# One inference step of a hybrid decoder: mLSTM and delta rule with tokens on partitions, head norms inside both

## The chip, the cores and the metric

The kernel runs on one core of a Trainium2 chip. The metric is the device time of one execution in microseconds. A core has TensorE for matrix products (PE in the profile, its weight loads PEld), VectorE (DVE), ScalarE (ACT), GpSimd (POOL) and a queue for transfers, SyncE (SP). Each engine works through its own instruction list; semaphores hold them together.

## The reference, cut to what matters

Two layers over a prompt of 1024 tokens and 8 sample sequences of 8 tokens, with the same weights. Layer 0 mixes with four mLSTM heads and four gated delta-rule heads; all in float32. The part around the change:

```python
# mLSTM, per chunk: b = cumsum(log f), m_t = running max
s = einsum('bthd,bshd->btsh', qc, kc) * exp(d - m_t)
num = einsum('btsh,bshv->bthv', s, vc) + a_inter * einsum('bthd,bhdv->bthv', qc, c)
den = sum(s, axis=2) + a_inter * einsum('bthd,bhd->bth', qc, n)
h = num / maximum(abs(den), exp(-m_t))
hm = rmsnorm(h, mi_norm) * sigmoid(mo)            # per head of 128
# delta rule, per chunk
v_new = u_c - w_c @ s
o = qd_c @ s + at_c @ v_new
s = exp(gl_c) * s + kd_c.T @ v_new
og = rmsnorm(o, gd_norm) * silu(gz)               # per head of 128
y = concatenate([hm, og]) @ w_out
```

## The kernel before

Activations lie transposed, features on the 128 partitions and the 1088 tokens (padded to TP = 1092) along the free dimension. Z has 20 such tiles: 0-3 the mLSTM queries and keys, 4-7 its values and then its outputs, 8-11 delta queries, 12-15 keys, 16-19 values and then outputs. Tokens go in 8 chunks of 128 (NC = 8) and one chunk of 64 for the sample group, which the code calls chunk NC. Layer 0 is a row of stages, and each stage ends with a barrier of all engines: products (input projection), mlstm, delta, headnorm, wout0 (output projection).

**mlstm** (L463) runs the prompt's chunks first and the sample chunk last. In each, TensorE makes the scores ST with the keys as weights, spreads three rows over the partitions (`bcast`, L527), turns the values (L551), and reads out with values as weights, so the outputs NUM come with features on partitions (L562, L564) and the denominator DEN, spread over all 128 partitions by a second set of products with ones (L569, L571). VectorE takes the maximum of the denominator and its bound, a reciprocal of 128x512 (L687) and the product (L689). For the sample chunk each product with a state is done for every sequence with 8 columns (L567, L574). The sample states are loaded by 20 transfers at the front (L498, L501) and stored by 20 at the end (L513, L516). Every buffer is single.

**delta** (L712) has a first part (preparation of all chunks, inverse of the 32x32 blocks on VectorE, sample group) and then a loop over the chunks. Its order on TensorE in chunk i: `new_values(i)` (L932, L937), `first(i + 1)` (L901), the state product SU (L954), `second(i + 1)` (L907, L910, L914), the outputs OUT (L961, L963) with `third(i + 1)` (L920) in their middle, `fourth(i + 1)` (L927). ScalarE turns WT and VN to SBUF (L1029, L1031) and scales the keys for the next chunk (`scaled`, L1021), which `fourth` wants. POOL makes the mask parts (`parts`, L1077), the spread inverses (L1087) and the keys at the chunk's end (L1061), which `first` and SU want. VectorE copies OUT to Z (L1197).

**headnorm** (L1603) makes for all 8 heads: squares on ScalarE (L1638), their sums over the partitions by products with a column that selects a row (L1651), root and reciprocal, the rows spread by products (L1659), two products per tile on VectorE (L1673, L1676), and the split in a high and a low half for the output projection (ScalarE L1643, POOL L1630). The gates come from DRAM in one transfer (L1622). The high halves go to Z 8-15, the low ones stay in Z 4-7 and 16-19. It also loads and splits the first weight of wout0.

## Time and profile before

| | |
|---|---|
| median of 3 runs | 4121.89 us (4121.21 to 4123.23) |
| the profiled execution | 4122.16 us, span 4120.4 us |
| PE / PEld busy | 88% / 81% of the span |
| DVE / ACT / POOL busy | 35% / 14% / 29% |
| mean granted PE clock | 0.895 of full |

The span is cut in stages by barriers, so a stage costs what the last of its engines costs, and a mean over the span tells little of it. The windows and the timeline show it stage by stage. A matmul of float32 shows as two records.

### The profile page before, as it was taken

Reading aid. Unit: us, or ns where it says so; the run is one execution under the profiler, and the core shown is the slowest. Engines: PE = TensorE matmul, PEld = TensorE weight load, DVE = VectorE, ACT = ScalarE, POOL = GpSimd, SP = SyncE. Lnnn points to the kernel's source line nnn. Section 1 sums busy time; section 2 is a strip of 40 time slices with the busy share of each in tenths; the row PEclk is TensorE's granted clock in tenths of the full one; section 3 lists DMA queues with packets and bytes.
Section 4 is the critical chain, followed back from the end, with each engine's and each line's share of the span. In section 5 each row is a group of like instructions: output and inputs, shape, how many; then the busy total and the mean of one; then the engine's idle time right before and its main releaser. Section 6 shows DMA issues by size and latency. Waiting matters only on the chain. (4 is left out here: it accounts for less than half of the span.)

```text
span 4120.4 us, 48469 instructions
## 1 busy us (share of the span) xinstructions
PE 3606.7 (88%) x20881; PEld 3348.4 (81%) x20881; DVE 1434.4 (35%) x2055; ACT 590.2 (14%) x982; POOL 1196.0 (29%) x545
## 2 busy tenths in 40 slices
PE   6999656889999999989885978799777899999998
PEld 6899555868999999988684768688555899999998
DVE  4931353533423241431001044555412342414143
ACT  4310111221100000011100023233111110000012
POOL 3433000325344344424030021111000444434442
PEclk8999875788999999999986889699755999999999
DMA  4112102212111111123113032100111211111111
GB/s 122 42 37 64 43 2 33 50 53 80 42 47 42 46 42 46 47 69 129 39 42 98 0 75 46 40 6 7 38 60 48 74 42 47 42 47 46 43 46 59
DMA packets 303612, 204.01 MB, mean 50 GB/s; under 512 B 73065, under 2 KB 283323, under 8 KB 302856
## 3 DMA queue, kind: packets, MB, share of 16 engines
q1 hardware_dynamic: 294056, 196.44, 16.6%
q10 hardware_dynamic: 9344, 4.47, 0.4%
q8 instruction: 165, 2.70, 0.3%
q14 instruction: 47, 0.39, 0.0%
HBM read 158.69 MB, written 33.40 MB: 47 GB/s over the span
## 5 line engine op out<-in xcount | busy, mean ns | idle before, releaser
L264 PE MATMUL ps<-u_r,wslots_r 128*128 128x364 f32 x4608 | 772.3, 330 | 0.0
L264 PEld LDWEIGHTS ps<-u_r,wslots_r 128*128 128x128 f32 x4608 | 770.8, 189 | 0.0
L264 PE MATMUL ps<-hn_r,wslots_r 128*128 128x364 f32 x2880 | 589.5, 331 | 11.7 <-PEq L76 11.7
L235 POOL TENSOR_TENSOR wslots_r<-rawm,sb_ones 128x1024 fp32r<-128x1024 f32 x133 | 321.2, 2415 | 912.8 <-PE ps L264 871.2
L264 PE MATMUL ps<-low_r,wslots_r 128*128 128x364 f32 x2688 | 543.6, 330 | 26.5 <-PEq L76 24.7
L264 PEld LDWEIGHTS ps<-hn_r,wslots_r 128*128 128x128 f32 x2880 | 497.1, 189 | 12.2 <-POOLq L229 12.2
L264 PEld LDWEIGHTS ps<-low_r,wslots_r 128*128 128x128 f32 x2688 | 462.0, 189 | 26.9 <-POOLq L229 24.8
L237 POOL TENSOR_TENSOR wslots_r<-rawm,wslots_r 128x1024 fp32r<-128x1024 f32 x133 | 379.1, 2851 | 10.4
L1685 DVE TENSOR_TENSOR xT<-xT,ps 128x1092 f32<-128x1092 f32 x80 | 103.4, 1292 | 667.6 <-PE ps L264 667.6
L1334 PE MATMUL ps<-hn_r,wslots_r 128*128 128x364 f32 x1392 | 278.3, 333 | 17.8 <-POOLq L1304 9.2
L1334 PEld LDWEIGHTS ps<-hn_r,wslots_r 128*128 128x128 f32 x1392 | 239.9, 191 | 24.3 <-DVE Z L1561 11.9
L2848 PE MATMUL ps<-xT 128*128 128x128 f32 (+7 forms) x1184 | 168.7, 287 | 1.9 <-DVE xT L3049 0.9
L2848 PEld LDWEIGHTS ps<-xT 128*128 128x128 f32 (+7 forms) x1184 | 152.1, 198 | 18.0 <-issue 8.7
L1334 PE MATMUL ps<-xT_r,wslots_r 128*128 128x364 f32 x696 | 155.1, 331 | 0.0
L1309 POOL TENSOR_TENSOR wslots_r<-raw,sb_ones 128x1024 fp32r<-128x1024 f32 x28 | 69.7, 2490 | 226.9 <-PE ps L1334 205.5
L1726 ACT ACTIVATE u_r<-u 128x1092 fp32r<-128x1092 f32 x32 | 35.8, 1118 | 628.3 <-DVE u L1723 628.3
L1726 ACT ACTIVATE low_r<-hn 128x1092 fp32r<-128x1092 f32 x32 | 35.8, 1118 | 627.8 <-DVE hn L1723 627.8
L1334 PEld LDWEIGHTS ps<-xT_r,wslots_r 128*128 128x128 f32 x696 | 122.6, 191 | 0.0
L2932 ACT ACTIVATE xT<-ps 128x512 f32<-128x512 f32 (+5 forms) x148 | 85.1, 598 | 172.3 <-DVE ps L3028 116.0
L264 PEld LDWEIGHTS ps<-Z_r,wslots_r 128*128 128x128 f32 x576 | 97.9, 192 | 9.6 <-POOLq L229 9.6
L264 PE MATMUL ps<-Z_r,wslots_r 128*128 128x364 f32 x576 | 98.2, 333 | 8.6 <-PEq L76 8.6
L1720 DVE TENSOR_TENSOR hn<-ps,row 128x1092 f32<-128x1092 f32 x32 | 41.5, 1296 | 184.0 <-PE ps L264 170.6
(576 smaller groups left out, 5108.2 us busy)
## 6 DMA issues: line engine op xcount, KB each, us to landing
rawm<-in_w_down SPq DMA_DIRECT2D x64, 512.0 KB
rawm<-in_w_up SPq DMA_DIRECT2D x63, 512.0 KB
raw<-in_w_in_even SPq DMA_DIRECT2D x28, 512.0 KB
xT<-x_saved SPq DMA_DIRECT2D x2, 4368.0 KB
xT<-in_cache_fox_kv SPq DMA_DIRECT2D x16, 512.0 KB
more_r<-more_r SPq DMA_DIRECT2D x28, 256.0 KB
panel_raw<-in_w_in_odd SPq DMA_DIRECT2D x6, 1024.0 KB
x_saved<-Z SPq DMA_DIRECT2D x1, 4368.0 KB
```

The costliest lines, as they stand in the source:

```text
L235: nc.gpsimd.tensor_tensor(r32(half[0][:, g % 2]), raw[:, g % 2], one, ALU.mult).then_inc(s["high"], 1)
L237: nc.gpsimd.tensor_tensor(r32(half[1][:, g % 2]), raw[:, g % 2], r32(half[0][:, g % 2]), ALU.subtract) \
L264: mm = pe.matmul(view[n % 2][:, c, :], r32(half[a][:, n % 2, k, :]), r32(t["x"][b][:, k, CH * c:CH * (c + 1)]), start=(k == 0 and (a, b) = ...
L1309: G_.tensor_tensor(r32(half[0][:, g % 2]), raw[:, g % 2], one, ALU.mult).then_inc(s["high"], 1)
L1334: mm = pe.matmul(acc[:, c, :], r32(half[a][:, g % 2, k, :]), r32((hn, low)[b][:, k, CH * c:CH * (c + 1)]), start=(k == 0 and (a, b) == HAL ...
L1685: return e.tensor_tensor(v3(xT[:, n, :]), v3(xT[:, n, :]), acc, ALU.add)
L1720: return e.tensor_tensor(v3(u[1][:, n, :]), acc, v3(row), ALU.mult)
L1726: return e.activation(r32(u[0][:, n, :]), u[1][:, n, :], ACT.Copy)
L2848: mm = pe.matmul(out(u, kind)[:, h, :], prob[0:r, n % 3, P * h:P * (h + 1)], v, start=(n == branch_first[(u, kind)] and h == 0), stop=(n = ...
L2932: nc.scalar.activation(prob[0:r, n % 3, :], S(n)[0:r], ACT.Exp).then_inc(act_.sem, act_.mark(("exp", n)))
```

## The change

Both mixers now give their outputs with the tokens on the partitions: in the read-out the decayed scores (and queries) are the weights, and values (and states) flow through. In mLSTM a 129th column of ones in the values gives the denominator in the same product. Norm, denominator and root are then factors of one column per head (128x4 for a chunk), by which a chunk is scaled; four transposes bring it back to features on partitions, where it meets its gate, comes from DRAM by chunk (18 slices in all), and is split in its high and low halves. The stage headnorm and its call are gone; the high halves lie in Z 0-3 and 8-11.

mLSTM is written anew: the sample chunk is first, buffers are double, the chunk i + 1 is prepared before chunk i is read out, sample states are updated two per chunk in the first four chunks and stored behind them. A state of 64 rows lies at partitions 0-63 or 64-127 and is multiplied there, without zero padding. For the sample chunk, queries are masked per sequence by POOL (`qm`), and states flow with 129 columns. The factor 0.125 of the keys goes into the input projection.

In delta, each chunk's squares, root and high half are on ScalarE, scaling and gating on VectorE, the transposes in `second`, the low half on POOL; the first weight of wout0 is loaded and split in its loop, and `keys_at_end(0)` stands behind the sample products on POOL.

```diff
-def mlstm(pr, I, O, C, Z, GC, RT, arena, ps):
...
+def mlstm(pr, I, O, C, Z, GC, RT, G, gam, blocks, bufs, ps):
...
+    order = [NC] + list(range(NC))
+    num = room([P, NC + 1, 4, P])
...
+            load_gate(0)
+            load_gate(1)
+            sp.wait_ge(dve_.sem, dve_.at(("Cb", NB - 1)))
+            for x in range(2):
+                sl = slice(64 * x, 64 * x + 64)
+                for b in range(NB):
+                    sp.dma_start(O["s_mlstm_c"][0, b].rearrange("(y x) d v -> x d y v", x=2)[x], Cb[sl, b, :, 0:P]).then_inc(s["st"], 16)
+                for y in range(2):
+                    sp.dma_start(O["s_mlstm_n"][0, :, 2 * y + x, :].rearrange("b (d o) -> d b o", o=1), Cb[sl, :, y, P:P + 1],
                                  allow_slow_non_contiguous=True).then_inc(s["st"], 16)
+            for k in range(2, 6):
+                load_gate(k)
...
+            for k in range(6, NC + 1):
+                load_gate(k)
+            sp.wait_ge(s["st"], 16 * 24)
...
+            def prepare(i):
+                k, r, cc = order.index(i), token_rows(i), cols(i)
+                if k:
+                    need(dve_, ("pt", order[k - 1]))
+                for h in hs4:
+                    m = pe.matmul(RB[:, h, 0:r], C["sel"][:, h, :], RT[:, cc], start=True, stop=True)
+                done(m, ("RB", i))
+                if k:
+                    need(act_, ("kt", order[k - 1]))
+                for h in hs4:
+                    pe.matmul(AB[hp(h), h // 2, 0:r], C["sel"][:, 4 + h, 0:64], RT[:, cc], start=True, stop=True)
+                for y in (0, 1):
+                    m = pe.transpose(TR[0:r, P * y:P * y + P], Z[:, 2 + y, cc], C["ident"][:])
+                done(m, ("TR", i))
+                if k:
+                    need(act_, ("vt", order[k - 1]))
+                for h in hs4:
+                    m = pe.transpose(VT[0:r, h, :], Z[:, 4 + h, cc], C["ident"][:])
+                done(m, ("VT", i))
+                need(dve_, ("D", i))
+                for h in hs4:
+                    m = pe.matmul(ST[0:r, h % 2, h // 2, 0:r], Z[hp(h), 2 + h // 2, cc], Z[hp(h), h // 2, cc], start=True, stop=True)
+                done(m, ("ST", i))
+
+            def read_out(i):
+                k, r = order.index(i), token_rows(i)
+                need(dve_, ("pt", i))
+                need(act_, ("vt", i))
+                need(dve_, "pad")
+                if k:
+                    need(dve_, ("num", order[k - 1]))
+                    need(act_, ("ssq", order[k - 1]))
+                else:
+                    need(dve_, "cols")
+                    need(dve_, "ends")
+                    pe.wait_ge(s["state"], 16 * 20)
+                    need(pool_, "qm")
+                p_, v_ = of(i, pt, pts), of(i, vt, vts)
+                if 0 < i < NC:
+                    need(dve_, ("C", i - 1))
                     need(dve_, ("qa", i))
+                for h in hs4:
+                    dst = N[h % 2][0:r, h // 2, :]
+                    m = pe.matmul(dst, p_[:, h, 0:r], v_[:, h, :], start=True, stop=not i)
+                    if 0 < i < NC:
+                        m = pe.matmul(dst, qa[hp(h), i % 2, h // 2, :], Cs[hp(h), i % 2, h // 2, :], start=False, stop=True)
+                    for b in range(NB if i == NC else 0):
+                        m = pe.matmul(dst, qm[hp(h), h // 2, b, :], Cb[hp(h), b, h // 2, :], start=False, stop=(b == NB - 1))
+                done(m, ("N", i))
...
+            prepare(NC)
+            need(dve_, "cols")
+            need(dve_, "ends")
+            prepare(0)
+            read_out(NC)
+            for i in range(NC):
+                if i + 1 < NC:
+                    prepare(i + 1)
+                if i < 4:
+                    update_sample(2 * i)
+                read_out(i)
+                update(i)
+                if i < 4:
+                    update_sample(2 * i + 1)
+                if i == 4:
+                    turn_back(0)
+                if i >= 4:
+                    turn_back(i - 3)
+            for k in range(5, NC + 1):
+                turn_back(k)
...
+            def squares(i):
+                k, r = order.index(i), token_rows(i)
+                need(dve_, ("num", i))
+                need(dve_, "clear")
+                for h in hs4:
+                    if h or k:
+                        need(act_, ("junk", k, h - 1) if h else ("ssq", order[k - 1]))
+                    ins = A.activation(junk[0:r], num[0:r, k, h, :], ACT.Square, accum_out=ssq[0:r, k, h:h + 1])
+                    step(("junk", k, h) if h < 3 else ("ssq", i), ins)
+
+            def root(n):
+                need(dve_, ("mean", n))
+                step(("root", n), A.activation(part[:, 5 * n:5 * n + 5 - n], part[:, 5 * n:5 * n + 5 - n], ACT.Sqrt))
...
+            prepare(NC)
+            prepare(0)
+            squares(NC)
+            for i in range(NC):
+                if i + 1 < NC:
+                    prepare(i + 1)
+                squares(i)
+                if i == 3:
+                    root(0)
+                if i == 4:
+                    high(0)
+                if i >= 4:
+                    high(i - 3)
+            root(1)
+            for k in range(5, NC + 1):
+                high(k)
...
+            def weigh(k):
+                r = token_rows(order[k])
+                pool.wait_ge(s[f"gate{k % 2}"], 16 * (k // 2 + 1))
+                step(("gate", k), E.tensor_tensor(gate[:, k % 2, :, 0:r], gate[:, k % 2, :, 0:r], spread(gam[:, 0:4], r), ALU.mult))
+            weigh(0)
+            weigh(1)
+            for k in range(NC + 1):
+                w = wide(order[k])
+                need(act_, ("high", k))
+                step(("low", k), E.tensor_tensor(r32(Z[:, 4:8, w]), Z[:, 4:8, w], r32(Z[:, 0:4, w]), ALU.subtract))
+                if k + 2 <= NC:
+                    weigh(k + 2)
...
+            def out(i):
+                k, r = order.index(i), token_rows(i)
+                need(pe_, ("N", i))
+                step(("den", i), V.tensor_copy(den[0:r, k].rearrange("p (y x o) -> p x y o", x=2, o=1), nums[0:r, :, :, P:P + 1]))
+                step(("num", i), V.tensor_copy(by_half(num[0:r, k]), nums[0:r, :, :, 0:P]))
+                need(dve_, ("den", i))
+                step(("minus", i), V.tensor_scalar(part[0:r, k], den[0:r, k], -1.0, None, ALU.mult))
+                need(dve_, ("minus", i))
+                step(("abs", i), V.tensor_tensor(den[0:r, k], den[0:r, k], part[0:r, k], ALU.max))
+                need(dve_, ("abs", i))
+                step(("bound", i), V.tensor_tensor(den[0:r, k], den[0:r, k], cols_of[0:r, i, 32:36], ALU.max))
+
+            def factors(n):
+                w = slice(5 * n, 5 * n + 5 - n)
+                need(act_, ("ssq", 3 + 4 * n))
+                need(dve_, ("bound", 3 + 4 * n))
+                step(("rden", n), V.reciprocal(den[:, w], den[:, w]))
+                need(dve_, ("rden", n))
+                step(("s1", n), V.tensor_tensor(part[:, w], ssq[:, w], den[:, w], ALU.mult))
+                need(dve_, ("s1", n))
+                step(("s2", n), V.tensor_tensor(part[:, w], part[:, w], den[:, w], ALU.mult))
+                need(dve_, ("s2", n))
+                step(("mean", n), V.tensor_scalar(part[:, w], part[:, w], 1.0 / P, EPS, ALU.mult, ALU.add))
+                need(act_, ("root", n))
+                step(("rroot", n), V.reciprocal(part[:, w], part[:, w]))
+                need(dve_, ("rroot", n))
+                step(("fac", n), V.tensor_tensor(fac[:, w], part[:, w], den[:, w], ALU.mult))
+
+            def scaled(k):
+                r = token_rows(order[k])
+                if k >= 2:
+                    need(pe_, ("HT", k - 2))
+                need(dve_, ("fac", 0 if k < 5 else 1))
+                step(("hs", k), V.tensor_tensor(hs[0:r, k % 2], num[0:r, k], spread(fac[0:r, k], P), ALU.mult))
+
+            def gated(k):
+                i = order[k]
+                r = token_rows(i)
+                need(pe_, ("HT", k))
+                need(pool_, ("gate", k))
+                step(("z", k), V.tensor_tensor(Z[:, 4:8, cols(i)], HT[:, :, 0:r], gate[:, k % 2, :, 0:r], ALU.mult))
...
+            for i in range(NC):
+                if i + 1 < NC:
+                    decay(i + 1)
+                if i < 4:
+                    state_sample(2 * i)
+                if i + 1 < NC:
+                    weights(i + 1)
+                out(i)
+                state(i)
+                if i < 4:
+                    state_sample(2 * i + 1)
+                if i == 3:
+                    factors(0)
+                    scaled(0)
+                    scaled(1)
+                if i == 4:
+                    gated(0)
+                    scaled(2)
+                if i >= 4:
+                    gated(i - 3)
+                    if i < 6:
+                        scaled(i - 1)
+            factors(1)
+            scaled(5)
+            scaled(6)
+            for k in range(5, NC + 1):
+                gated(k)
+                if k + 2 <= NC:
+                    scaled(k + 2)
...
+            sp.wait_ge(s["out"], 16)
+            first_load(sp, s, W, following)
+            for k in range(NC + 1):
+                if k >= 2:
+                    sp.wait_ge(dve_.sem, dve_.at(("z", k - 2)))
+                if k == NC:
+                    sp.wait_ge(dve_.sem, dve_.at(("S", NC - 1)))
+                    sp.dma_start(O["p_gdn_s"][0, 0].rearrange("h k v -> k h v"), S[:, NC % 2]).then_inc(s["last"], 16)
+                i = order[k]
+                sp.dma_start(gate[:, k % 2, :, 0:token_rows(i)], G[4:8, :, cols(i)].rearrange("h p t -> p h t")).then_inc(s[f"gate{k % 2}"], 16)
+            sp.wait_ge(s["last"], 16)
...
+                if i >= 2:
+                    turn_back(i - 2)
...
+            def turn_back(k):
+                r = token_rows(order[k])
+                need(dve_, ("hs", k))
+                if k:
+                    need(dve_, ("z", k - 1))
+                if k + 1 < NC:
+                    need(dve_, ("S", k + 1))
+                for h in hs:
+                    m = pe.transpose(HT[:, h, 0:r], turned[0:r, k % 2, h, :], C["ident"][0:r, 0:r])
+                done(m, ("HT", k))
...
                 if i:
                     need(dve_, ("S", i - 1))
+                if i >= 2:
+                    need(dve_, ("z", i - 2))
                 for h in hs:
                     m = pe.matmul(SU[:, h], kd[:, i % 2, h], vn[:, h], start=True, stop=True)
                 done(m, ("SU", i))
                 if more:
                     second(i + 1)
                 if i:
-                    need(dve_, ("O", i - 1))
+                    need(dve_, ("hs", i - 1))
+                to = OUT[(i + 1) % 2]
                 for h in hs:
-                    m = pe.matmul(OUT[:, h], vn[:, h], at[:, i, h], start=True, stop=not i)
+                    m = pe.matmul(to[:, h], at[:, i, h], vn[:, h], start=True, stop=not i)
                     if i:
-                        m = pe.matmul(OUT[:, h], S[:, i % 2, h], Z[:, 8 + h, cols(i)], start=False, stop=True)
+                        m = pe.matmul(to[:, h], Z[:, 8 + h, cols(i)], S[:, i % 2, h], start=False, stop=True)
                     if h == 1 and more:
                         third(i + 1)
...
+            for k in range(NC - 2, NC + 1):
+                turn_back(k)
...
+            def root(k):
+                i = order[k]
+                r = token_rows(i)
+                need(pe_, ("O", i))
+                need(dve_, "clear")
+                for h in hs:
+                    need(act_, ("square", k, h - 1) if h else ("square", k - 1, 3) if k else "VT")
+                    step(("square", k, h), A.activation(junk[0:r], OUT[k % 2][0:r, h, :], ACT.Square, accum_out=ssq[0:r, k, h:h + 1]))
+                need(act_, ("square", k, 3))
+                step(("root", k), A.activation(ssq[:, k], ssq[:, k], ACT.Sqrt, scale=1.0 / P, bias=eps[:, 0:1]))
+
+            def high(k):
+                w = wide(order[k])
+                need(dve_, ("z", k))
+                step(("high", k), A.activation(r32(Z[:, 8:12, w]), Z[:, 16:20, w], ACT.Copy))
...
+                root(i)
+                if i >= 2:
+                    high(i - 2)
                 if i + 1 < NC:
                     scaled(i + 1)
...
-            need(act_, ("kk", NC - 1))
-            need(dve_, ("last", NC - 1))
-            keys_at_end(0)
...
+            need(act_, ("kk", NC - 1))
+            need(dve_, ("last", NC - 1))
+            need(pe_, ("SUb", NB - 1))
+            keys_at_end(0)
...
+            def low(k):
+                w = wide(order[k])
+                need(act_, ("high", k))
+                step(("low", k), G_.tensor_tensor(r32(Z[:, 16:20, w]), Z[:, 16:20, w], r32(Z[:, 8:12, w]), ALU.subtract))
...
+                if i == 2:
+                    pool.wait_ge(s["out"], 16)
+                    first_split(nc, pool, s, W)
+                if i >= 3:
+                    low(i - 3)
...
+            def scaled(k):
+                i = order[k]
+                r = token_rows(i)
+                need(act_, ("root", k))
+                step(("rroot", k), V_.reciprocal(fac[:, k], ssq[:, k]))
+                need(dve_, ("rroot", k))
+                if k == 0:
+                    dve.wait_ge(s["out"], 16)
+                if k >= 2:
+                    need(pe_, ("HT", k - 2))
+                step(("hs", k), V_.tensor_tensor(turned[0:r, k % 2], OUT[k % 2][0:r], spread(fac[0:r, k], P), ALU.mult))
+
+            def gated(k):
+                i = order[k]
+                need(pe_, ("HT", k))
+                dve.wait_ge(s[f"gate{k % 2}"], 16 * (k // 2 + 1))
+                r = token_rows(i)
+                step(("z", k), V_.scalar_tensor_tensor(out=Z[:, 16:20, cols(i)], in0=HT[:, :, 0:r], scalar=gam[:, 4:5], in1=gate[:, k % 2, :, 0:r],
+                                                       op0=ALU.mult, op1=ALU.mult))
...
-                need(pe_, ("O", i))
-                step(("O", i), V_.tensor_copy(Z[:, 16:20, cols(i)], OUT))
...
+                if 1 <= i < NC - 1:
+                    gated(i - 1)
+                scaled(i)
...
+                    if mlstm_of.get(g) in (2, 3):
+                        step(("free", what), V.scalar_tensor_tensor(out=v3(dst), in0=acc, scalar=0.125, in1=v3(row[:]), op0=ALU.mult, op1=ALU.mult))
+                    else:
+                        step(("free", what), V.tensor_tensor(v3(dst), acc, v3(row[:]), ALU.mult))
...
-def head_norms(pr, I, Z, which, G, gates, arena, W, following, ps):
...
-            with nc.sbuf_tensor("normroom", [P, 2300], F32) as normroom:
-                head_norms(pr, I, Z, which, G, hn[:], Arena(wslots[:, 1].rearrange("p k m -> p (k m)"), spare[:], RT[:], normroom[:]), W, last, ps)
...
```

## Rows read from the trace of the kernel before

**Rows 1.** Windows: start:end, length, busy us of PE, PEld, DVE, ACT, POOL, clock, DMA share, GB/s

```profile
452.30:606.80 154.50, 86.53 (x608) 81.92 (x608) 84.19 (x157) 27.93 (x65) 0.00 (x0) 0.79 0.04 8
606.80:671.10 64.30, 49.95 (x246) 44.78 (x246) 22.41 (x73) 2.68 (x8) 0.00 (x0) 0.50 0.00 1
671.10:696.60 25.50, 0.00 (x0) 0.00 (x0) 0.00 (x0) 0.00 (x0) 0.00 (x0) 0.50 0.53 41
...
885.60:956.10 70.50, 46.79 (x96) 20.41 (x96) 31.00 (x18) 20.09 (x18) 30.80 (x10) 0.65 0.20 74
...
834.50:879.40 44.90, 42.98 (x353) 41.04 (x353) 20.67 (x40) 9.44 (x25) 14.47 (x13) 1.00 0.00 1
```

**Rows 2.** Timeline, mlstm: start, duration, engine, line, idle before and its releaser

```profile
452.34 5.24 SPq L498 DMA_DIRECT2D xT<-in_state_mlstm_c  x8
...
471.09 0.60 DVE L638 COPY xT<-Z 64x256 f32<-64x256 f32 x2
...
486.42 3.35 DVE L687 RECIPROCAL wslots<-wslots 128x512 f32<-128x512 f32 x1
...
490.41 0.60 DVE L638 COPY xT<-Z 64x256 f32<-64x256 f32 x2
```

**Rows 3.** Timeline of one chunk in the loop of delta

```profile
834.56 0.49 PE L937 MATMUL ps<-xT,hn 128*128 128x128 f32 x2 [0.46 <-ACT hn L1029]
...
836.43 0.60 ACT L1031 ACTIVATE hn<-ps 128x512 f32<-128x512 f32 x1 [1.92 <-PE ps L937]
836.57 2.16 POOL L1087 TENSOR_TENSOR hn<-xT,sb_block 128x512 f32<-128x512 f32 x2 [3.80 <-PE ps L937]
...
840.05 1.16 PE L914 MATMUL ps<-hn,Z 128*128 128x128 f32 x8
...
841.35 2.62 POOL L1077 TENSOR_TENSOR Z<-xT,sb_level 128x512 f32<-128x512 f32 x2 [1.51 <-PE ps L914]
...
843.93 1.16 PE L927 MATMUL ps<-hn,Z 128*128 128x128 f32 x8
...
845.77 0.49 PE L937 MATMUL ps<-xT,hn 128*128 128x128 f32 x2 [0.46 <-ACT hn L1029]
...
847.44 1.06 PE L901 MATMUL ps<-hn,Z 128*128 128x128 f32 x8
```

**Rows 4.** Timeline at the end of delta and the start of wout0

```profile
884.89 0.69 DVE L1197 COPY Z<-ps 128x512 f32<-128x512 f32 x1 [0.66 <-PE ps L963]
887.51 2.12 ACT L1638 ACTIVATE normroom<-Z 128x1092 f32<-128x1092 f32 x2 [5.65 <-PEq L76]
...
956.15 44.03 PE L264 MATMUL ps<-Z_r,wslots_r 128*128 128x364 f32 x250 [8.57 <-PEq L76]
```

**Rows 5.** Groups of instructions, shapes apart: count, total us, mean ns, idle before

```profile
L421 ACT ACTIVATION_READ_ACCUMULATOR Z<-Z 128x1 f32 x8 | 1.5, 193 | 0.0
L607 ACT ACT_TABLE_LOAD x1 | 1.3, 1283 | 0.0
...
L607 ACT ACTIVATE xT<-xT,GC 128x128 f32<-128x128 f32 x32 | 10.2, 390 | 2.4 <-DVE xT L644 2.4
...
L680 DVE SCALAR_TENSOR_TENSOR xT<-xT,ps 64x129 f32<-64x129 f32 x28 | 9.8, 349 | 27.9 <-PE ps L581 27.2
...
L685 DVE TENSOR_TENSOR wslots<-wslots 128x512 f32<-128x512 f32 x8 | 5.5, 692 | 0.3
...
L1119 DVE COPY xT<-hn 128x4 f32<-128x4 f32 x8 | 1.3, 162 | 0.0
...
L1050 POOL TENSOR_TENSOR Z<-Z,hn 128x512 f32<-128x512 f32 x8 | 10.2, 1276 | 23.7 <-PE ps L829 23.7
```

**Rows 6.** Transfers by line: count, KB each, us from issue to landing

```profile
out_s_gdn_s<-wslots SPq DMA_DIRECT2D x1, 2048.0 KB, 10.0
...
xT<-delta_inverse SPq DMA_DIRECT2D x16, 64.0 KB, 2.2
```

**Rows 7.** Timeline, delta: 128-row products followed by 64-row ones

```profile
705.31 0.39 PE L828 MATMUL ps<-Z 128*128 128x128 f32 x2
...
705.54 0.39 PE L829 MATMUL ps<-Z 128*128 128x128 f32 x2
...
705.85 0.67 PE L836 MATMUL ps<-hn,Z 64*64 64x64 f32 x8
```

567 lines of the change are left out of this document (251 added, 316 removed).

## The prediction

> **What bounds the kernel now.** I read four views, in this order. First the windows of layer 0's mixers. In each, the reader is to see how little of the stretch TensorE is busy, and at which clock [rows 1]. The mLSTM chunks take 154.5 us with PE busy 86.5; the sample group 64.3 us at clock 0.50; then 25.5 us pass with no engine busy, while only the stores of the sample state leave; the stage of head norms takes 70.5 us. Elsewhere PE is the bound (the delta loop: 43.0 of 44.9 us busy at clock 1.00). Second, the timeline of one mLSTM chunk [rows 2]: L638 starts at 471.09 and again at 490.41, so a chunk takes 19.3 us, and 3.35 us of it are one reciprocal of 128x512. It is a chain with no overlap: PE stands still while VectorE ends a chunk. Third, the timeline of one chunk of the delta loop [rows 3]: L937 starts at 834.56 and at 845.77, a period of 11.21 us, PE nearly without gaps. Fourth, the end of that stage [rows 4]: its last copy ends at 885.58, the next stage's first instruction starts 1.93 us later (what a stage boundary costs), and the output projection's first matmul starts at 956.15.
>
> So what counts is what ends last in each stage: in mLSTM the dependency chain, in the delta loop PE, in head norms everything, since nothing of another stage runs beside it. Stages are barriers, so each one's saving adds to the others.
>
> **mLSTM, front.** The state loads come first, as now: eight issues take 5.24 us [rows 2], 0.655 each. 21 of them (20 and the new block mask) are 13.8 us, and a transfer of 64 KB lands 2.2 us after issue [rows 6]: ready at 452.3+16.0 = 468.3. PE's own front (row ends, 9 transposes, the preparation of the sample chunk and of chunk 0) is some 90 records. A pair of records runs at a pitch of 0.23 us at full clock [rows 7], 0.46 at half; with the front starting at half and two waits on Exp and mask it takes until about 471. I take 471: here the two ends are almost equal.
>
> The sample chunk's read-out is 72 records (8 of weights by values, 64 of queries by state) instead of two sets of 64+8 now. At 0.115 us each it is 8.3 us, at half clock 16.6; today's sample group runs at 0.50 throughout [rows 1]. I take 11.5, a little nearer to full since 129 columns flow instead of 8: it ends at 482.5.
>
> **mLSTM, the loop.** Now chunks overlap: PE prepares i+1 before it reads out i. I follow the cycle from one read-out's end to the next's, by durations [rows 3, 5]. VectorE: denominator copy 0.16, numerator copy 0.69, three tiny steps (0.24 each with their own wait, an estimate from the 0.16 of a 128x4 copy plus a semaphore) 1.57 in all; state update, two of 0.35, 0.70; then 0.70 for a sample state (first four chunks) or 1.4 for gate and scale of an earlier chunk (last four); the next mask 0.69. PE: score products 8 records, 0.9; one sample product 0.5 (first four); read-out 16 records, 1.85. Seven hand-overs of 0.07 make 0.5. The head rows are at partitions 0-63 or 64-127, so products of 64 rows alternate with ones of 128. Where the trace changes so, L829's pair starts at 705.54 and L836 at 705.85, 0.31 against the pair's pitch of 0.23 [rows 7]: 0.08 to 0.09 per change, nine of them on the cycle, 0.8. Sum: 8.3 and 8.5; I take 8.45. PE's own work is some 58 to 66 records and switches, 7.5 us, so it lies just below: the cycle, not PE, sets the pace. ScalarE per chunk: Exp 1.3, two copies 1.0, four squares with accumulation. Each accumulation adds an extra read of 0.19 [rows 5]: 0.39+0.19+0.06 = 0.64, four are 2.6; with the high half 0.6, in all 5.5 of 8.45 us: covered by about 2 us. Eight chunks: 67.6 us, to 550.1.
>
> The factors of the first five chunks come in the fourth: reciprocal and three tiny steps 0.7, table load 1.28 [rows 5], root, two more steps, two scalings of 0.69; less what overlaps the updates, 4.1 us, to 554.2.
>
> **mLSTM, the end.** After the last read-out: copy 0.9, squares 2.6, factors 1.9 (5.4); scaling, transposes and gate of the sixth 2.1 (7.5); only then is the gate of the eighth requested: issue 0.4 and 2.2 landing (10.2), weighting on POOL 1.28 [rows 5] (11.5). From there POOL is the queue: low 6, weight 8, low 7 and low 8 at 1.3 each, with the ninth gate's load and ScalarE's high half in between, 16.8 in all: 571.0. With a boundary of 1.93: 573. The stores of the sample state (13 us of issues) now leave beside chunks 4 to 6; on the SP queue the gates of the third chunk and later stand behind them, and are wanted about 15 us after, so the cover is 0 to 3 us. The delta stage started at 696.6. **Saved: 123.6 us.**
>
> **Delta.** POOL's first key product now stands behind the last sample product: mask parts late by 0.6 us at most; I take 0.6. In the loop the copy of 0.69 is replaced by a gate of 0.69 and scaling 0.9 on VectorE, busy 20.7 of 44.9 us before: hidden. The transposes, 4 records, stand on PE between L910 and L914, which started the moment its input was there, and everything behind is back to back [rows 3]: 0.46 per chunk, seven times, 3.2. Swapped operands of the output change no count. On ScalarE the squares and root (2.9) and the high half (0.6) are put ahead of the beta-keys (1.26): from 837.03, the end of L1031, this is 841.8, wanted by L927 at 843.93: hidden by 2.1. On POOL the low half is put ahead of the mask parts and waits for ScalarE's high half at 840.5: low 1.3, parts 2.6, L1087 2.2 give 846.6, wanted by L901 at 847.44 plus the 0.46: hidden by 1.2 only. The two splits of the first weight (4.7 us) fall in POOL's slack early in the loop, behind the landing of the 2 MB state; about 10 us of slack by the same count.
>
> The end: last output, then squares and root 2.9, scaling 0.9 (3.8), the seventh's gate, transposes 0.6 and the last gate 0.7 (6.1), high half 0.65, low half 1.3: 8.1. The last gate's load, issued when the seventh of nine is gated, lands at 4.6: hidden. Before, PE's last output ended near 884.9; now 884.9+0.6+3.2+8.1 = 896.8, boundary to 898.7.
>
> **Head norms.** The stage goes whole: 70.5 us [rows 1]. Its first weight and gates are loaded elsewhere, as counted. The output projection starts at 898.7 in old time instead of 956.15. **Saved with delta's cost: 57.4 us.** Folding the factor 0.125 into another operation of the same size in the products is nothing.
>
> Sum: 123.6+57.4 = 181.0. The profiled execution took 4122.16 us (span 4120.4), the median is 4121.89: **3941 us**.
>
> A rule that speaks against this change is weighed: the Trainium skill, TensorEngine Tiling (Array Packing), Tiling Modes, Key Properties, says a change of tiling mode drains the array. The trace agrees in kind, with 0.08 us beyond the pitch.
>
> **Rivals.**
> A: the clock stays at half in mLSTM, as 0.79 and 0.50 now show [rows 1]. Score and read-out products and switches double: 3.3 us per chunk, 26 us: 3967. Against: gaps of 7 us shrink to under 2, and the delta loop with such gaps has 1.00.
> B: POOL's low half is slowed by VectorE beside it and its parts come late in delta: 2 us over the slack of 1.2, six times, 12: 3953.
> C: every switch costs the whole drain: a pair's duration 0.39 less its pitch 0.23 is 0.16 instead of 0.08; nine switches by 0.08, eight chunks, 6: 3947. This is how far the rule on draining goes at its strictest.
> D: chunks of mLSTM don't overlap, because one wait joins them (the read-out waits for the squares of the chunk before). A chunk then costs 19.3 less the reciprocal, 16, against 8.45: 60 more, 4001.
> E, the other side: the 18 gate slices are on the path, each requested only when a buffer is free. The 64 KB row says 2.2 us; the change loses once a slice costs over 2.2+181/18 = 12.3 us that nothing covers, and at 13 it gives 4135. The 2 MB store's landing is the only row that is that long [rows 6].
> F: the stage's work merely moves, and nothing is saved (4122): against it stands that stores, the wide reciprocal and the 8-row matmuls vanish.
>
> **How the numbers follow.** Forecast 0.58 (own range 3922 to 3958: sample read-out 8.3 to 16.6, loop cycle 7.5 with PE as bound to 9.5, end 14 to 20); A 0.13, B 0.11, C 0.10, D 0.05, E 0.02, F 0.01. The range 3918 to 3970 holds forecast, A, B, C less their tails, about 0.8 to 0.85. The measurement tells about 0.2% (8 us) from no change. Faster 0.97, same 0.01, slower 0.02.
>
> **What would show it.** The mLSTM stage some 119 us long with read-outs 8 to 9 us apart; clock near 1.00 in its loop; no idle 25 us behind it; a delta period of 11.7 us, with L901 not waiting for POOL; 11 us from the last output to the stage's end; no stage between it and the projection. I am wrong if the mLSTM loop waits on ScalarE (accumulations) or SP (gates), or if the front waits longer for the state.

## The result

The changed kernel takes 3958.61 us, the median of 4 runs (3956.04 to 3968.01), against 4122.44 (4121.21 to 4123.23) for the kernel before: a ratio of 0.9606, 95% interval 0.9593 to 0.9618. It saves 163.8 us where 181.0 were forecast. The profiled execution took 3960.81 us, its span 3959.0. Between the two profiled executions 161 us are saved: the mLSTM stage goes from 244.3 [rows 1] to 138.9 us, the stage of head norms (70.5) is gone, and delta takes 203.9 us where it took 189.0 (from 696.6 to the 885.6 of [rows 1]).

The windows of the changed kernel, with the columns of [rows 1]: the mLSTM stage in six pieces (front, sample read-out, the chunks while TensorE has work, the step to the fifth chunk, chunks 5 to 7, the end), delta in four, and the start of the output projection.

```profile
452.00:468.70 16.70, 12.27 (x86) 10.44 (x86) 4.85 (x16) 5.47 (x13) 3.77 (x4) 0.60 0.37 81
468.70:485.65 16.95, 16.95 (x72) 14.28 (x72) 0.00 (x0) 0.00 (x0) 0.00 (x0) 0.50 0.10 23
485.65:517.70 32.05, 32.05 (x259) 24.48 (x258) 18.22 (x55) 14.78 (x56) 5.34 (x8) 0.91 0.01 2
517.70:530.50 12.80, 9.90 (x65) 7.19 (x64) 6.71 (x21) 6.42 (x17) 0.00 (x0) 0.80 0.42 60
530.50:566.40 35.90, 28.30 (x151) 20.89 (x150) 14.45 (x36) 11.08 (x40) 9.05 (x8) 0.69 0.49 38
566.40:591.10 24.70, 6.51 (x29) 4.26 (x28) 9.24 (x22) 6.26 (x15) 9.78 (x8) 0.50 0.28 38
591.10:683.30 92.20, 89.17 (x572) 85.00 (x572) 53.61 (x149) 36.09 (x104) 21.67 (x20) 0.70 0.24 57
683.30:694.00 10.70, 6.45 (x27) 5.63 (x28) 4.73 (x8) 0.00 (x0) 9.88 (x8) 0.50 0.74 204
694.00:784.00 90.00, 83.84 (x673) 80.06 (x672) 42.22 (x83) 33.14 (x117) 44.60 (x37) 0.97 0.12 29
784.00:795.00 11.00, 3.91 (x32) 3.25 (x31) 4.94 (x11) 5.02 (x18) 5.07 (x4) 0.84 0.18 48
```

The mLSTM stage ends at 591.15 (the first transfer of delta) instead of 573; the projection starts at 795.02, 203.9 us later, where 202.1 were forecast (I set delta's own length by [rows 3, 4]). So 18 of the 20 us that the two stages miss lie in mLSTM. Two things are to be seen there. While the chunks flow (third row), PE is busy for 32.05 of 32.05 us: PE sets the pace. And from 530.5 on it no longer does, the clock falls to 0.69 and 0.50, and the DMA share is 0.49 while only 38 GB/s move.

The timeline of that place: SP's queue with the stores (L535, L537, L545) and the requests for gate slices (L528), POOL's weighting of a slice L754, and VectorE's product with it L867 (columns as in [rows 2]). A gate slice is one chunk's part of the gates, 256 KB; slice 0 is the sample chunk's.

```profile
529.95 2.08 SPq L535 DMA_DIRECT2D out_s_mlstm_c<-xT  x3
...
532.08 3.67 SPq L537 DMA_DIRECT2D out_s_mlstm_n<-xT  x2
...
535.78 13.49 SPq L528 DMA_DIRECT2D hn<-gate_tiles  x3
...
547.05 1.04 POOL L754 TENSOR_TENSOR hn<-hn,gam 128x512 f32<-128x512 f32 x1 [12.77 <-DMA hn<-gate_tiles]
...
548.20 0.69 DVE L867 TENSOR_TENSOR Z<-ps,hn 128x512 f32<-128x512 f32 x1 [5.42 <-POOL hn L754]
...
570.20 0.61 SPq L545 DMA_DIRECT2D out_p_mlstm_n<-xT  x1
...
570.85 12.44 SPq L528 DMA_DIRECT2D hn<-gate_tiles  x3
...
581.07 1.04 POOL L754 TENSOR_TENSOR hn<-hn,gam 128x512 f32<-128x512 f32 x1 [9.74 <-DMA hn<-gate_tiles]
```

Gate slice 2 is requested at 535.78, behind the 20 stores of the sample state (16 of 64 KB, L535, and 4 of single four-byte elements, L537), and POOL can use it at 547.05, 11.3 us later. Slice 6, behind the four stores of the prompt's state, needs 10.2 us. (In delta, where no such store is about, a slice of the same size lands in 3.0 us by the transfers' rows.) VectorE stands 5.42 us in the gate of a chunk that could wait, with the work of chunk 6 queued behind it. The state product L623 (keys by values) comes once in each chunk, behind its read-out, so its starts mark the chunks 0 to 7. They are 492.97, 501.20, 509.44, 517.67, 530.45, 540.91, 557.61 and 566.36: steps of 8.24 three times, then 12.8 (to chunk 4), 10.5 (chunk 5), **16.7** (chunk 6) and 8.75, and 24.8 to the end of the stage.

The first three pairs of a read-out in the loop, eight in all from 514.33 on, and the state product behind it; then one head of the sample read-out:

```profile
514.33 0.49 PE L611 MATMUL ps<-xT,hn 128*128 128x129 f32 x2
514.75 0.49 PE L613 MATMUL ps<-xT,hn 64*128 64x129 f32 x2
515.17 0.49 PE L611 MATMUL ps<-xT,hn 128*128 128x129 f32 x2
...
517.67 0.66 PE L623 MATMUL ps<-xT,hn 128*64 128x129 f32 x8
```

```profile
468.69 0.66 PE L611 MATMUL ps<-xT,hn 128*64 128x129 f32 x2 [3.67 <-DMA xT<-in_state_mlstm_n]
469.29 3.69 PE L615 MATMUL ps<-xT,hn 64*64 64x129 f32 x16
472.92 0.69 PE L611 MATMUL ps<-xT,hn 128*64 128x129 f32 x2
```

L611 is p v with 128 rows, L613 q C with 64. From one pair of records to the next it takes 0.42 us, where a pair without a change of rows takes 0.22 to 0.23 [rows 7]: 0.20 for each change, not 0.08. It is 0.42 at each of the eight pairs, whether the next one adds to the same result (L611 to L613) or not (L613 to L611), so the shared result isn't what costs. The read-out takes 3.34 us where 1.85 plus switches were counted. In the sample read-out a record takes 0.23, at half clock from end to end.

### The profile page after: what moved, and what is told of

It is laid out like the page before. It is cut to its first block and busy times, and to the rows that moved or that the text cites. A ratio compares the mean times of both kernels' runs of the same rounds, so it can differ in the third digit from the quotient of the medians.

```text
span 3959.0 us, 48131 instructions
## 1 busy us (share of the span) xinstructions
PE 3541.1 (89%) x20622; PEld 3293.8 (83%) x20622; DVE 1354.6 (34%) x1978; ACT 606.4 (15%) x1124; POOL 1207.5 (31%) x574
```

## The experiments

For each kernel the three places that matter, in us; the rest is what the unchanged part behind the projection's start takes to the end of the span. A ratio is to the kernel before, run on the same chip.

| kernel | first L623 | mLSTM ends | projection starts | delta | rest | median | ratio, 95% |
|---|---|---|---|---|---|---|---|
| changed | 492.97 | 591.15 | 795.02 | 203.9 | 3164.0 | 3958.6 | 0.9606 (0.9593-0.9618) |
| e1 | 491.35 | 574.22 | 775.34 | 201.1 | 3160.5 | 3940.1 | 0.9568 (0.9552-0.9584) |
| e2 | 492.02 | 574.23 | 773.15 | 198.9 | 3167.9 | 3946.1 | 0.958 (0.9564-0.9596) |
| e3 | 492.51 | 584.19 | 783.09 | 198.9 | 3161.6 | 3946.0 | 0.9576 (0.956-0.9592) |
| e4 | 481.29 | 579.88 | 782.13 | 202.3 | 3163.5 | 3947.3 | 0.9576 (0.956-0.9592) |
| e5 | 490.88 | 568.41 | 772.22 | 203.8 | 3163.5 | 3938.2 | 0.9566 (0.9551-0.958) |
| e6 | 489.92 | 596.06 | 796.22 | 200.2 | 3166.1 | 3957.1 | 0.9611 (0.959-0.9631) |
| e7 | 492.72 | 589.39 | 789.23 | 199.8 | 3162.6 | 3954.4 | 0.9598 (0.9583-0.9612) |
| e8 | | 738.51 | 937.32 | 198.8 | 3163.9 | 4106.1 | 0.9976 (0.9966-0.9986) |
| e9 | 481.84 | 553.06 | 751.45 | 198.4 | 3160.9 | 3910.7 | 0.9497 (0.9484-0.951) |
| e10 | 490.57 | 584.61 | 783.50 | 198.9 | 3164.7 | 3951.0 | 0.9582 (0.9567-0.9597) |
| e11 | 476.44 | 546.63 | 746.50 | 199.9 | 3169.2 | 3911.9 | 0.9488 (0.9475-0.9501) |
| e12 | 479.01 | 556.54 | 756.79 | 200.3 | 3160.2 | 3924.9 | 0.9523 (0.9508-0.9538) |

Read the two columns "delta" and "rest" first. They are of one profiled execution each. Delta's code is the same in all but four rows (e7, e9, e11, e12, by one order on POOL), and its time goes from 198.8 to 203.9. The rest is the same in all, and goes from 3160.2 to 3169.2. So a whole time can't tell 5 us, and the effects below are read from the stage that was edited.

**e1: all gate slices early.** My theory against the rival that POOL's and VectorE's chain makes chunk 6 long.

```diff
-            load_gate(0)
-            load_gate(1)
+            for k in range(NC + 1):
+                load_gate(k)
...
-            for k in range(2, 6):
-                load_gate(k)
```

> All nine gate slices of the mLSTM stage get buffers of their own and are loaded before the state stores. Theory Q (the slices stand behind the stores in the DMA queues): nothing waits for a slice any more, chunk 6 falls from 16.7 to about 8.5 us and chunk 5 from 10.5 to about 9.5, the end of the stage from 24.8 to about 18; together 12 to 18 us less, a time near 3944. Rival V (the chain over POOL and VectorE sets those chunks, the DMA wait only hides it): chunk 6 stays above 12 us and the time falls by 5 at most, to 3954 or more.

Measured: state products 516.06, 529.36, 540.85, 548.56, 555.60, so chunk 6 takes 7.7 us instead of 16.7, and the end is 18.6 instead of 24.8. The stage ends 16.9 us earlier, 15.3 of it counted from its first state product. I had expected chunk 5 to shrink to 9.5, and it did not: it took 11.5 (10.5 in the changed kernel). For chunk 6 and the end theory Q holds and the rival is out.

**e2: without the stores of the vectors n.** Which of the stores in front of the slices is it? The outputs for n are left out.

```diff
-                for y in range(2):
-                    sp.dma_start(O["s_mlstm_n"][0, :, 2 * y + x, :].rearrange("b (d o) -> d b o", o=1), Cb[sl, :, y, P:P + 1],
-                                 allow_slow_non_contiguous=True).then_inc(s["st"], 16)
...
-                sp.dma_start(O["p_mlstm_n"][0, 0].rearrange("(y x) (d o) -> x d y o", x=2, o=1)[x], Cs[sl, NC % 2, :, P:P + 1],
-                             allow_slow_non_contiguous=True).then_inc(s["st"], 16)
```

> Leaves out the six stores of the state vectors n (elements of 4 bytes, four of the sample, two of the prompt); the C stores and the two ring buffers of the gate stay as they are. Theory E (the packets of 4 bytes hold the queues): slice 2 lands about 4 us after its issue and slice 6 in 3, chunk 6 falls to about 11 us, the end to about 19; 8 to 12 us less in all, near 3949. Rival B (the bytes of the C stores hold them): slice 2 still needs 8 us or more, and at most 3 us go, 3955 or more.

Measured: slice 2 is requested at 531.68 and usable at 534.58, 2.9 us later, chunk 6 takes 7.7 us, and the stage ends at 574.23, as with e1, though the slices again stand behind 1 MB of C stores. That is more than theory E said: the stores of n, 8 KB beside 1 MB, are the whole effect. The transfers between 515 and 592 us, in 40 slices of 1.9 us (busy tenths and GB/s), first of the changed kernel and then of e2:

```profile
DMA  0003454999995985605000005000190356214000
GB/s 0 9 0 68 102 102 36 92 14 15 27 94 20 51 24 30 156 4 136 0 0 0 0 0 138 2 0 0 35 45 10 47 27 118 64 17 119 0 0 0
```

```profile
DMA  0014444415500024001400151055000079992001
GB/s 9 0 28 98 100 100 100 99 20 136 136 0 9 0 21 119 0 0 20 121 0 0 34 134 37 0 140 136 0 0 0 17 178 320 294 276 44 13 13 29
```

At half busy (4 and 5) the engines move about 100 GB/s of C stores. In the changed kernel they are then full, with 14, 15 and 27 GB/s in the ninth to eleventh of these slices of time, 530.4 to 536.2. What is under way there is told by the queue's packets (packets started in the window, MB, share of the 16 engines' time; a packet's whole time is put down to the window in which it starts, so a share can exceed 100%). First the changed kernel in four windows (521 to 526, 526.2 to 528.1, 530 to 536 and 538 to 545), then e2 from 532.5 to 536.5:

```profile
q1 hardware_dynamic: 1017, 0.46, 44.3%
q1 hardware_dynamic: 1161, 0.05, 37.5%
q1 hardware_dynamic: 277, 0.13, 132.6%
q1 hardware_dynamic: 414, 0.21, 75.5%
```

```profile
q1 hardware_dynamic: 1056, 0.52, 51.9%
```

By these rows, worked out as a mean, a packet of a C store takes 0.035 us (0.443 of 16 times 5 us, over 1017). The first two stores of n, 1024 four-byte elements, leave between 526.2 and 528.1 (1161 packets, but only 0.05 MB), and at 0.010 us a packet they are quick. It is the packets that start afterwards that are slow: 0.46 us each from 530 to 536, with 0.13 MB in 277 packets, so nearly all of them of C stores. The second 1024 elements leave around 537, and behind them the packets of the gate slices take 0.20 us each, where those of e2 take 0.031. So the four-byte stores hold the engines by what they do to the packets of some 6 to 7 us behind them. Why they do is not shown.

**e10: the slices from another queue.** Does a slice wait for what stands before it in SP's queue, or for the 16 DMA engines?

```diff
-            for k in range(2, 6):
-                load_gate(k)
...
-            for k in range(6, NC + 1):
-                load_gate(k)
...
+                if k + 2 <= NC:
+                    j = order[k + 2]
+                    act.dma_start(gate[:, k % 2, :, 0:token_rows(j)], G[0:4, :, cols(j)].rearrange("h p t -> p h t")).then_inc(s[f"gate{k % 2}"], 16)
```

> The changed kernel with the gate slices 2 to 8 requested from ScalarE's queue, each right after the high half that frees its buffer; two buffers, and all stores as they are. Theory O (a slice waits only for what stands before it in its own queue): slice 2 lands about 3 us after its issue, chunk 6 falls from 16.7 to about 8.5 us and the stage ends 13 to 16 us earlier, 3943. Rival S (the stores of 4-byte elements hold the 16 DMA engines, whatever the queue): slice 2 needs 7 us or more, the stage ends at most 5 us earlier, 3954 or more.

```profile
531.12 0.39 ACTq L708 DMA_DIRECT2D hn<-gate_tiles  x1
...
542.63 1.04 POOL L753 TENSOR_TENSOR hn<-hn,gam 128x512 f32<-128x512 f32 x1 [9.93 <-DMA hn<-gate_tiles]
```

Requested at 531.12 on ScalarE's queue, usable at 542.63: 11.5 us again. Counted from the end of the last store's issue (535.75 in the changed kernel, 531.30 here) the slice is usable after 11.3 us in both. Theory O is out. Of rival S the first sign is met (7 us or more) and the second is not: the stage ends 6.5 us earlier, not 5 at most, and the time is 3951.0, not 3954 or more. Of these 6.5 us 2.4 come ahead of the first state product, where the code is the same. Of the other 4.1 half is that the stores' issues ended 2 us sooner after it, the rest I did not trace.

The packets say what holds the slice. ScalarE's queue is q10, SP's is q1; first from 534.6 to 535.2, then from 535 to 542:

```profile
q1 hardware_dynamic: 649, 0.00, 64.7%
q10 hardware_dynamic: 116, 0.06, 82.9%
```

```profile
q10 hardware_dynamic: 1008, 0.50, 97.9%
q1 hardware_dynamic: 17, 0.00, 0.1%
```

The Trainium skill (DMA: Bandwidth & Descriptors, Queues, rings and completion order) says an engine goes round the queues that have work, a packet at a time. The trace agrees: in the 0.6 us in which both queues have work, they start packets side by side, 116 and 649 of them. But from 535 on SP's queue has next to nothing left, and the packets of slices 2 and 3 still take 0.109 us each, until 542, against 0.031 in e2. So in this stretch the slice stands behind nothing in a queue; its own packets are slow. That its first packet starts only at 534.6, 3.5 us after the request, isn't explained.

**e3: read-outs with two changes of tile.**

```diff
-                for h in hs4:
-                    dst = N[h % 2][0:r, h // 2, :]
-                    m = pe.matmul(dst, p_[:, h, 0:r], v_[:, h, :], start=True, stop=not i)
-                    if 0 < i < NC:
-                        m = pe.matmul(dst, qa[hp(h), i % 2, h // 2, :], Cs[hp(h), i % 2, h // 2, :], start=False, stop=True)
...
+                if 0 < i < NC:
+                    for h, first in ((0, 1), (1, 1), (0, 0), (1, 0), (2, 0), (3, 0), (2, 1), (3, 1)):
+                        start = first == (h < 2)
+                        a, w = (p_[:, h, 0:r], v_[:, h, :]) if first else (qa[hp(h), i % 2, h // 2, :], Cs[hp(h), i % 2, h // 2, :])
```

> The read-out of a prompt chunk does the same eight pairs in another order: p v of heads 0 and 1, q C of heads 0 to 3, p v of heads 2 and 3, so two changes between 128-row and 64-row matmuls within it in place of seven. Theory S (each change costs 0.19 us): a read-out of 3.34 us falls to about 2.4, the period of the first four chunks from 8.24 to about 7.3, and the later ones by up to 1 us each; 4 to 6.5 us less, 3952 to 3955. Rival (the pitch of 0.42 us belongs to these matmuls whatever stands beside them): 3.3 us and no change, 3958.

```profile
504.24 2.00 PE L613 MATMUL ps<-xT,hn 128*128 128x129 f32 x16
...
506.17 0.66 PE L628 MATMUL ps<-xT,hn 128*64 128x129 f32 x8
```

(These lines are L611 and L623 of the changed kernel, moved by the edit.) The same 16 records now take 1.93 us instead of 3.34, and the period of the first chunks is 6.83 instead of 8.24: 1.41 less per chunk, more than the 0.95 expected. The rest fits with the four q C products running two and two beside each other, as in e4: that would save four records of 0.11, an estimate. Theory S holds. But of the 8.9 us gained up to chunk 5 (532.01 instead of 540.91) only 4.1 were left at chunk 6 (553.54 instead of 557.61), a step of 21.5 us, because the slice came when it came. The stage ended 7.0 us earlier.

**e4: sample products in alternating pairs.**

```diff
-                    for b in range(NB if i == NC else 0):
-                        m = pe.matmul(dst, qm[hp(h), h // 2, b, :], Cb[hp(h), b, h // 2, :], start=False, stop=(b == NB - 1))
...
+                    for b in range(NB):
+                        for h in (2 * y, 2 * y + 1):
+                            m = pe.matmul(N[h % 2][0:r, h // 2, :], qm[hp(h), h // 2, b, :], Cb[hp(h), b, h // 2, :], start=False, stop=(b == NB - 1))
```

> In the read-out of the samples the 64 products of 64 rows alternate between the two heads of a pair, so that neighbours use different row halves and different banks. Theory O (neighbours on the two row halves overlap): the read-out falls from 16.95 us to about 9, the time by 7 to 8, to 3951. Rival (they run one after the other in either order): 17 us as before and no change, 3958.

```profile
468.86 1.09 PE L616 MATMUL ps<-xT,hn 128*64 128x129 f32 x4 [3.52 <-DMA xT<-in_state_mlstm_n]
469.88 3.71 PE L619 MATMUL ps<-xT,hn 64*64 64x129 f32 x32
473.52 1.12 PE L616 MATMUL ps<-xT,hn 128*64 128x129 f32 x4
474.57 1.98 PE L619 MATMUL ps<-xT,hn 64*64 64x129 f32 x32
476.48 1.16 PE L573 MATMUL ps<-RT,sb_sel 128*128 128x128 f32 x8
```

7.6 us instead of 16.95. At half clock a record takes 0.116 instead of 0.23: neighbours on different row halves, with results in different banks, run beside each other. The edit changes both at once, so whether the row halves alone would do it isn't shown. The second half is at full clock. The Trainium skill (TensorEngine Tiling (Array Packing), Tiling Modes, Key Properties) says that different tiles work in parallel; the trace agrees, once neighbours in the order are on different tiles. The stage ended 11.3 us earlier, 2.5 of it because the next preparation now meets full clock (7.3 us at 0.62 in the changed kernel, 4.8 at 1.00 here).

**e5: the factors late** (on top of e1).

```diff
+                if i == 4:
+                    factors(0)
+                    scaled(0)
+                    scaled(1)
                 out(i)
...
-                if i == 3:
-                    factors(0)
-                    scaled(0)
-                    scaled(1)
```

> On top of e1 (all gate slices loaded early), the factors of the first five chunks and their two scalings stand behind the mask and weights of chunk 5 on VectorE, and their root behind the Exp of chunk 5 on ScalarE. Theory F (in the changed kernel TensorE stands idle for 2.9 us and falls to half clock because the mask of chunk 5 waits behind the factors): the step of 13.3 us between the fourth and fifth state product of e1 falls to about 9, the stage ends 4 us earlier, 3936. Rival (the factors only move their 4 us in front of the fifth chunk's outputs, and chunk 5 grows by what the step before loses): the two steps together stay at 24.8 us, as in e1 (3940).

The step is 7.65 us where e1 has 13.30, the next one 11.37 (e1 11.49): both together 19.0 against 24.8, and the stage ends 5.8 us earlier. Theory F holds. In the whole time it isn't seen (3938.2 and 3940.1), since this run had delta at 203.8 and e1 at 201.1.

**e6 and e12: no preparation ahead.** Rival D put a price of 60 us on chunks that don't overlap. The cut is TensorE's list; ScalarE's and VectorE's are changed in the same way.

```diff
             for i in range(NC):
-                if i + 1 < NC:
-                    prepare(i + 1)
...
                 update(i)
...
+                if i + 1 < NC:
+                    prepare(i + 1)
```

> The changed kernel with the preparation of chunk i + 1 put behind chunk i's read-out, updates and squares on TensorE, ScalarE and VectorE; the same instructions in another order. My theory P: the overlap hides only waits, a chunk takes about 11 us instead of 8.24, 15 to 22 us more in all, 3973 to 3981. Rival D of the prediction (without overlap a chunk costs 16 us): 60 us more, 4018.

> e9 without its late factors and with the serial order of e6. Theory W (in e6 the missing overlap cost only 5 us because the waits for gate slices absorbed the rest; with them gone it shows): the state products are 9 to 10 us apart against 6.83, the stage ends 18 to 26 us later than in e9, 3929 to 3937. Rival N (the overlap is worth little by itself): at most 10 us, 3921 or less.

e6: the products are 9.9, 10.9, 9.1, 14.2, 11.4, 16.0 and 10.7 us apart, 8.8 us more in all; the stage ends 4.9 us later, and the time (3957.1) can't be told from the changed kernel's. Both my price and D's were too high. I then supposed that the waits for slices had absorbed the cost. e12, without those waits, says no:

```profile
479.00:500.50 21.50, 20.62 (x211) 16.07 (x210) 14.36 (x44) 10.90 (x42) 5.26 (x7) 1.00 0.01 2
```

Three periods of 7.2 us, PE busy 20.62 of 21.50 at clock 1.00. e9, with the preparation ahead, has 6.83. The stage ends 3.5 us later than in e9. As e9 has the late factors besides, and e5 gave 5.8 us for these, no cost of the order is left to be seen at the stage's end. Rival N holds: in the first chunks the preparation ahead is worth 0.4 us each at full clock. In the first three steps of e6 it was 1.7 on average, but there the granted clock was 0.84, 0.76 and 0.94 where the changed kernel had 1.00, so that number is of order and clock together. Neither run is rival D itself: in the serial order, too, PE prepares i + 1 while VectorE and ScalarE finish i, so the chunks still overlap, and what a full loss of overlap costs is not measured.

**e7: mask parts first in delta.**

```diff
-            need(act_, ("kk", NC - 1))
-            need(dve_, ("last", NC - 1))
-            need(pe_, ("SUb", NB - 1))
-            keys_at_end(0)
...
             parts(0)
+            need(act_, ("kk", NC - 1))
+            need(dve_, ("last", NC - 1))
+            need(pe_, ("SUb", NB - 1))
+            keys_at_end(0)
```

> In delta, POOL makes the mask parts of the first chunk before its keys, in place of after. Theory K (the keys, put behind the last sample product, hold the first chunk's parts): the first product of the loop starts 1 to 2.5 us sooner after the stage's start than the 96.7 us of the changed kernel. Rival: the same stage, unchanged, begins its loop between 93.8 and 96.7 us after its start in the runs so far, with the clock; nothing is seen beyond that, and the time stays at 3958.

The loop's first product starts 94.2 us into the stage, which is within what the unchanged code shows, 93.8 to 96.7. Counted from the end of the last sample state on VectorE the spread goes away: 3.45 us in the changed kernel and in e1 to e6, e8 and e10, 2.78 in e7, e9, e11 and e12. So the order on POOL costs 0.7 us. The prediction had 0.6.

**e8: delta's part alone.** The old mLSTM, a norm stage for its four heads, the new delta.

```diff
-            mlstm(pr, I, O, C, Z, GC, RT, G, gam, more[:, 0:NB * NS], [flat, hflat, wflat, row[:]], ps)
+            mlstm(pr, I, O, C, Z, GC, RT, Arena(flat, wflat, row[:]), ps)
+            head_norms(pr, I, Z, [4, 5, 6, 7], G, hn[:, 0:4], gam, Arena(flat), ps)
```

> One part of the change alone: the old mLSTM stage, the head norms stage for its four heads alone (half the tiles, no first weight), and the new delta stage with its norms inside. If the parts add (theory): the mLSTM stage takes its 244 us, the norm stage about 40 (70.5 before for eight heads), delta to projection 204 as in the changed kernel, so 105+40 us above the changed kernel, 4104. Rival: a stage for four heads costs nearly what one for eight does (its chain of root and first and last tile), 55 or more, and this part alone brings nothing: 4119 or above.

4106.1 us, 0.24% less than before. The norm stage for four heads takes 46.0 us (its first transfer 692.47, delta's 738.51), against 70.5 for eight [rows 1]: between the theory and its rival. So this part alone saves about 10 us of the 164 by the ratio (19 between the two profiled executions; the eight runs of e8 lie between 4100.9 and 4115.7), and only together does the norm stage go.

**e9: all of it, and e11.** e1, e3, e4, e5 and e7 together; e11 also issues the loads of n from ScalarE.

> All gate slices early, grouped read-outs (the p v and q C products ordered so that two changes remain), sample products in alternating pairs, the factors late, and POOL's mask parts of delta's first chunk ahead of its keys. If the gains add: e1 gave 16.9 us at the end of the mLSTM stage, the pairs 9.3, the grouped read-outs 1.4 per chunk for the four chunks with TensorE full (5.6) and some of it later, the factors 4, the parts 1: about 37 us off 3958, so 3921. Rival (another chain than TensorE's, VectorE's cycle, takes over once TensorE is relieved, so the grouped read-outs and the factors give little): 3930 or more.

> e9 with the four loads of the sample's state vectors n (elements of 4 bytes) issued by ScalarE at the front of the stage in place of SP between the C loads. Theory O: the state is there 3 us or more earlier, TensorE's wait of 3.5 us at the sample's read-out goes, 3907. Rival S (the packets take the same engines, wherever they are issued): the state is there when it was, 3911.

```profile
481.80:502.30 20.50, 20.50 (x211) 16.07 (x210) 15.03 (x46) 10.89 (x42) 4.72 (x7) 1.00 0.00 1
502.30:534.40 32.10, 25.14 (x211) 20.22 (x210) 20.51 (x57) 17.30 (x57) 9.06 (x8) 0.88 0.41 34
534.40:553.00 18.60, 6.59 (x29) 4.30 (x28) 9.34 (x22) 6.26 (x15) 9.77 (x8) 0.59 0.04 8
```

e9: 3910.7 us, 0.9497 of before, by the ratios 45 us less than the changed kernel, where 37 were expected. At the stage's end it is 38.1; the rest is delta at its short end (198.4, of which e7's order explains 0.7) and 3 us behind it. PE is still full in the first chunks, so the rival (VectorE's cycle) did not take over. In e11 PE no longer waits for the state, the read-out starts at 464.94 where e9's starts at 469.19, and the stage ends 6.4 us earlier. Theory O of this run holds. The four loads of n leave at the front, beside SP's issues and not between them; the run changes the queue and the time of issue together and can't tell which of the two helps. In the whole time it doesn't show (its rest took 3169.2), and whether e11 beats e9 stays open.

## Why the prediction was right, and where it was off

The verdict and the size held: 3941 was forecast, 3958.6 measured, in the range of 3918 to 3970. It is just beyond the forecast's own range (3922 to 3958), and lies in the wider range, which was drawn for the rivals A (3967), B (3953) and C (3947) too; of these only the mechanism of C was seen. Some sums of the prediction are off by little: the terms of the loop's cycle add up to 8.2 and 8.4, not 8.3 and 8.5, ScalarE's slack is 3 us and not 2, and the own range begins at 3927 by its parts. Step by step, measured less forecast:

- **Front: −2.3.** "Ready at 468.3" was right, the wait ended at 468.69. That PE's own front takes until 471 was not: it was done at 465.0.
- **Sample read-out: +5.45** (16.95, forecast 11.5). The term took a clock nearer to full "since 129 columns flow", which no row supported; the row of before said 0.50 for such a stretch [rows 1], and so it was. The upper bound, 16.6, was the answer.
- **Loop, first chunks: 8.24 against 8.45, for the wrong reason.** "The cycle, not PE, sets the pace" failed: PE is full. A step holds 71 or 72 records, not 58 to 66. A change of tile costs 0.20 and not 0.08, which is rival C and a little beyond; the other records of 64 rows or columns were cheaper than counted (eight pass in about 0.6 us, where 0.9 was taken for the scores). The errors cancelled, and that is luck.
- **Factors: 4.6 against 4.1.** Right. That they could wait (e5) I did not see.
- **Chunks 5 and 6, and the end: +10 and +6.** This is the step that failed: "on the SP queue the gates of the third chunk and later stand behind them, and are wanted about 15 us after, so the cover is 0 to 3 us". It took 2.2 us for the landing, from a row of 64 KB where a slice has 256 KB [rows 6]; that alone is small, 3.0 us in delta. The changed kernel and e10 show 11.3 and 11.5 us behind the four-byte stores, e2 shows 2.9 without them, and e1 that nothing is left of chunk 6's excess once the slices come first. The row that would have told stood in front of me: the same 20 stores alone held the stage of before for 25.5 us [rows 1], of which 20 issues of 0.655 explain 13 at most. Rival E had the mechanism but priced it over all 18 slices; it struck two.
- **Delta: +1.8**, with its term of 3.2 for the transposes at 7 times 0.24 in fact (period 11.45 against 11.21 before), 8.0 for the tail (8.1), and a first product that comes 0.7 us late by e7. The tail agrees though one part of it does not: the last slice was to be hidden, and VectorE waited 1.39 us for it. The stage's own variation of 5 us covers what is left.

A (half clock in the loop) did not come: 0.91, and 1.00 once it flows. But each long wait brought half clock behind it, at 0.69 and 0.50. B did not come: the period is 11.45. ScalarE's squares, feared at 0.64, have a pitch of 0.40 in delta and 0.43 in mLSTM: the accumulator's read starts before its own square's record ends, and the next square starts behind it. D did not come either: the chunks overlap. Its price is not measured (e6).

This last point changes the explanation, too. The prediction said the chain of 19.3 us [rows 2] becomes 8.45 because chunks now overlap. By e6 the order of the code brings 4.9 us of a stage of 139, by e12 at most 3.5 us of 105. What can be seen to have shrunk is the work on the chain: VectorE worked 84.2 us for the eight chunks of before [rows 1] and 18.2 for four now, sample states included, so 10.5 and 4.6 a chunk. How much of the stage's 105 us is due to the columns in place of 128x512 maxima and reciprocals, how much to the double buffers and to the samples' place at the front, no run here separates.

## What to carry to other kernels

Before a small transfer is put on the path, look at what the DMA engines are doing at that time, not at the queue it stands in: a few KB of stores in four-byte elements ahead of it cost it 8 us here, and another queue did not bring it in sooner. A gain made ahead of such a wait is lost in it (e3), so take the wait out first. And where matmuls of 64 rows stand among those of 128, order them in blocks, alternating the halves, and the banks of their results, inside a block: that was worth 1.4 us per read-out and 9 us in the sample's.

## What was not expected of the hardware

- In the read-out a change between 128-row and 64-row matmuls costs 0.20 us at full clock, beside a record's 0.11.
- Neighbouring 64-row matmuls on different halves and banks take 0.116 us per record at half clock instead of 0.23.
- 1024 four-byte elements are stored within 1.9 us, and for some 6 us behind them the packets of other transfers are slow: 0.46 us each for C stores (0.035 before), 0.11 to 0.20 for gate slices (0.031 without such stores), in whichever queue they are. A slice was usable after 11.3 and 11.5 us instead of 2.9.
- Identical code in the delta stage took 198.8 to 203.9 us; the start of its last sample state lies 89.2 to 92.1 us into the stage. What sets it isn't shown: the changed kernel and e7 have the same code up to there, and 92.1 and 90.3.
